# First block: the output projection from rounded halves, in one stage with the second norm

## The reference, cut to what matters

```python
    for i, z in enumerate(branches):
        gate = jax.nn.sigmoid(p[..., GATE_OFF + i * D_MODEL:GATE_OFF + (i + 1) * D_MODEL])
        term = gate * (z @ w_branch[i])
        y = term if y is None else y + term
    return y @ w_out
...
        x = x + mod[2] * _mixer_merge(p, ml_x, *mix_args)
        h = _modulate(_rmsnorm(x, norm2_g[l]), mod[3], mod[4])      # h * (1 + scale) + shift
        x = x + mod[5] * _peer(h, *peer_args)
```

## Time and profile before

| | |
|---|---|
| median of three runs | 4560.39 us (4550.98 to 4560.59) |
| the profiled execution | 4564.81 us, span 4563.0 us |
| TensorE busy | 4219.2 us (92%) |
| DVE busy | 2528.1 us (55%) |
| ScalarE busy | 1668.1 us (37%) |
| POOL busy | 453.7 us (10%) |
| mean DMA rate | 169 GB/s |
| mean granted TensorE clock | 0.952 of full |

### The profile page before, as it was taken

The page is one execution under the profiler, slowest core; times in us unless marked ns, Lnnn a source line. Parts: engine busy times, 40 slices in busy tenths (PEclk is TensorE's granted clock), DMA queues, the critical chain, the costliest instruction groups (busy, mean ns, idle before and its releaser), DMA issues. The chain is left out here.

```text
span 4563.0 us, 62458 instructions
## 1 busy us (share of the span) xinstructions
PE 4219.2 (92%) x25458; PEld 3636.0 (80%) x25458; DVE 2528.1 (55%) x5099; ACT 1668.1 (37%) x2099; POOL 453.7 (10%) x130
## 2 busy tenths in 40 slices
PE   5899889999999999999979798999998988898788
PEld 4777468888887888888778598998887977887687
DVE  4635359766661344444475477764666645553664
ACT  2333133333332322222245244444444433443453
POOL 1222024300000000000034150000000012000000
PEclk7999989999999999999989899999998989998999
DMA  6421123445558765555444355778886511545164
GB/s 220 157 92 60 72 76 120 138 148 185 185 177 306 239 211 186 202 185 201 160 126 133 134 167 182 247 249 283 284 287 216 163 44 56 153 158 165 56 188 136
DMA packets 453479, 769.75 MB, mean 169 GB/s; under 512 B 20389, under 2 KB 324741, under 8 KB 432937
## 3 DMA queue, kind: packets, MB, share of 16 engines
q1 hardware_dynamic: 452554, 763.65, 50.0%
q10 hardware_dynamic: 640, 2.11, 0.1%
HBM read 662.31 MB, written 103.38 MB: 168 GB/s over the span
## 5 line engine op out<-in xcount | busy, mean ns | idle before, releaser
L113 PE MATMUL bank<-hThi_l,pr_whi 128*128 128x512 f32 (+1 forms) x2304 | 788.7, 342 | 30.9 <-DVE pr_wlo L1787 15.7
L113 PE MATMUL bank<-hTlo_l,pr_whi 128*128 128x512 f32 (+1 forms) x2304 | 777.8, 338 | 0.0
L113 PE MATMUL bank<-hThi_l,pr_wlo 128*128 128x512 f32 (+1 forms) x2304 | 777.8, 338 | 0.0
L113 PE MATMUL bank<-pr_whi,pr_ahi 128*128 128x512 f32 x1536 | 600.8, 391 | 10.0 <-DVE pr_alo L1886 9.7
L1692 ACT ACTIVATE pr_whi<-pr_w 128x2048 fp32r<-128x2048 f32 x270 | 515.5, 1909 | 245.3 <-DMA pr_w<-peer_v_in 237.8
L113 PE MATMUL bank<-pr_whi,pr_alo 128*128 128x512 f32 x1536 | 599.3, 390 | 0.0
L113 PE MATMUL bank<-pr_wlo,pr_ahi 128*128 128x512 f32 x1536 | 599.3, 390 | 0.0
L113 PEld LDWEIGHTS bank<-hThi_l,pr_whi 128*128 128x128 f32 x2304 | 440.7, 191 | 81.2 <-DVE pr_wlo L1787 17.1
L113 PEld LDWEIGHTS bank<-hThi_l,pr_wlo 128*128 128x128 f32 x2304 | 440.4, 191 | 45.6
L113 PEld LDWEIGHTS bank<-hTlo_l,pr_whi 128*128 128x128 f32 x2304 | 441.1, 191 | 43.3
L1872 DVE TENSOR_TENSOR pr_a<-pr_gs,pr_g 128x1024 f32<-128x1024 f32 (+1 forms) x128 | 122.7, 959 | 489.8 <-DMA pr_g<-dense_weights 489.8
(11 more groups left out here) (545 smaller groups left out, 8296.6 us busy)
## 6 DMA issues: line engine op xcount, KB each, us to landing
pr_w<-peer_u_in SPq DMA_DIRECT2D x128, 1024.0 KB, 5.7
pr_w<-peer_v_in SPq DMA_DIRECT2D x128, 1024.0 KB, 5.0
dense_weights<-pr_buf SPq DMA_DIRECT2D x12, 4096.0 KB, 17.0
gu_w<-ffn_w_up_in SPq DMA_DIRECT2D x88, 512.0 KB, 4.8
gr_w<-w_in_in SPq DMA_DIRECT2D x32, 1024.0 KB, 5.3
expert_scores<-pr_s SPq DMA_DIRECT2D x64, 512.0 KB, 6.8
pr_gs<-expert_scores SPq DMA_DIRECT2D x64, 512.0 KB, 5.9
pr_g<-dense_weights SPq DMA_DIRECT2D x64, 512.0 KB, 7.1
```

What stands on the lines that cost most here:

```text
L113: ins = pe.matmul(psum, a, b, start=first and i == 0, stop=last and i == len(terms) - 1)
```

## The change

`project` and `norm` between mixing and retrieval are replaced by one stage, `merge_out`. y and w_out become pairs of halves. w_out is cut into four quarters of 256 columns, and a product tile is one quarter by one row tile: 16 tiles in layer 0, 8 in layer 1. The four quarters are fetched at the end of the mixing stage; the high halves of quarters 0 and 1, the low half of quarter 0 and the high halves of y are made there too, the others in the new stage. TensorE does quarters 0 and 1 for all row tiles first, then quarters 2 and 3 row tile by row tile; behind each row tile DVE and ScalarE norm it, while TensorE goes on. The shift and scale rows are fetched when the first half of the tiles is ready; the gain and the weights of the retrieval stage at the stage's start.

In the mixing stage:

```diff
-                for n in range(11, n_w):
+
+                fetch_branch(11)
+                sp.wait_ge(gate_psum, halves_n - 4)
+                fetch_out(0, out_in0)
+                fetch_branch(12)
+                sp.wait_ge(gate_psum, halves_n - 2)
+                fetch_out(1, out_in1)
+                fetch_branch(13)
+                sp.wait_ge(gate_psum, halves_n)
+                fetch_out(2, out_rest)
+                sp.wait_ge(gated, n_it)
+                fetch_out(3, out_rest)
+                for n in range(14, n_w):
                     fetch_branch(n)
                 sp.wait_ge(mod_in, 32)
+                sp.wait_ge(out_rest, 32)
+                sp.wait_ge(out_lo, 1)
...
+                pool.wait_ge(out_hi, 1)
+                pool.tensor_tensor(room.lo[0], room.raw[0], room.hi[0].bitcast(F32), ALU.subtract).then_inc(out_lo, 1)
...
+                    if i == halves_n - 1:
+                        act.wait_ge(out_in0, 16)
+                        act.activation(room.hi[0], room.raw[0], ACT.Copy).then_inc(out_hi, 1)
...
+                act.wait_ge(out_in1, 16)
+                act.activation(room.hi[1], room.raw[1], ACT.Copy).then_inc(out_hi, 1)
+                for o in range(KD):
+                    act.wait_ge(added, halves_n - 16 + o + 1)
+                    act.activation(room.y_hi[:, o, t0:TALL], yT[:, o, t0:TALL], ACT.Copy)
```

`fetch_out(n, landed)` fetches quarter n of w_out, 1 MB, into `room.raw[n]`. The new stage (its opening and small helpers are cut; `bank` cycles through PSUM banks 0 to 3, `turn_bank` through 4 to 7):

```diff
+def merge_out(K, l, x, y, room, mod2, gain2, hT, tiles, streams, ahead):
...
+    items = [(n, t) for n in range(2) for t in tiles] + [(n, t) for t in tiles for n in range(2, 4)]
+    half = 2 * n_t
...
+        @block.sync
+        def _(sp):
+            sp.dma_start(gain2, K.dram["norm2_g"][l:l + 1, :].broadcast_to([P, D])).then_inc(gain_in, 16)
+            ahead.fetch(sp, first_in, rest_in)
+            sp.wait_ge(ready, half)
+            for c in (1, 0):
+                for s in streams:
+                    sp.dma_start(room.mods[:, c, s, :], K.ada[l, s:s + 1, (3 + c) * D:(4 + c) * D].broadcast_to([P, D])).then_inc(mods_in, 16)
+            ahead.land(sp, first_in, rest_in)
...
+            def high_terms(i):
+                n, t = items[i]
+                if n:
+                    pe.wait_ge(w_low, n)
+                if i >= 4:
+                    pe.wait_ge(freed, i - 3)
+                for k in range(KD):
+                    left = y_hi[:, k, t * P:(t + 1) * P]
+                    pe.matmul(bank(i), left, room.hi[n][:, k, :], start=k == 0, stop=False)
+                    pe.matmul(bank(i), left, room.lo[n][:, k, :], start=False, stop=False)
+
+            def low_term(i):
+                n, t = items[i]
+                for k in range(KD):
+                    if i == 0:
+                        pe.wait_ge(y_low, k + 1)
+                    last = pe.matmul(bank(i), y_lo[:, k, t * P:(t + 1) * P], room.hi[n][:, k, :], start=False, stop=k == KD - 1)
+                last.then_inc(ready, 1)
+
+            def turn(j):
+                for g in range(2 * j, 2 * j + 2):
+                    pe.wait_ge(scaled, g + 1)
+                    if g >= 4:
+                        pe.wait_ge(lo_done, g - 3)
+                    for c in range(4):
+                        at = (4 * (g % 2) + c) * P
+                        last = pe.transpose(turn_bank(g)[:, c, :], h[:, j % 2, at:at + P], K.ident[:, :])
+                    last.then_inc(turned, 1)
+
+            high_terms(0)
+            high_terms(1)
+            low_term(0)
+            low_term(1)
+            for i in range(2, len(items)):
+                high_terms(i)
+                low_term(i)
+                j, odd = divmod(i - half, 2)
+                if j >= 2 and not odd:
+                    turn(j - 2)
+            for j in range(n_t - 2, n_t):
+                turn(j)
...
+            def split_hi(n):
+                act.activation(room.hi[n], room.raw[n], ACT.Copy).then_inc(w_high, 1)
+
+            def square(j):
+                act.wait_ge(added, half + 2 * j + 2)
+                act.activation(h[:, j % 2, :], x[:, tiles[j], :], ACT.Square, scale=D ** -0.5, accum_out=ss[:, j:j + 1]).then_inc(squared, 1)
+
+            def root(j):
+                act.wait_ge(shifted, j + 1)
+                act.activation(ss[:, j:j + 1], ss[:, j:j + 1], ACT.Sqrt).then_inc(rooted, 1)
+
+            def hi_of(j):
+                for g in range(2 * j, 2 * j + 2):
+                    act.wait_ge(turned, g + 1)
+                    at = place(g)
+                    act.activation(hT[0][:, at[0], at[1]], turn_bank(g), ACT.Copy).then_inc(hi_done, 1)
+
+            split_hi(2)
+            split_hi(3)
+            ahead.split_hi(act, first_in, ahead_hi)
+            for j in range(n_t):
+                if j >= 2:
+                    hi_of(j - 2)
+                square(j)
+                root(j)
+            for j in range(n_t - 2, n_t):
+                hi_of(j)
...
+            def split_lo(n):
+                if n >= 2:
+                    dve.wait_ge(w_high, n - 1)
+                dve.tensor_tensor(room.lo[n], room.raw[n], room.hi[n].bitcast(F32), ALU.subtract).then_inc(w_low, 1)
+
+            def take(i):
+                n, t = items[i]
+                dve.wait_ge(ready, i + 1)
+                if i >= 4:
+                    dve.wait_ge(added, i - 3)
+                part = K.junk[:, i % 4 * 256:(i % 4 + 1) * 256]
+                dve.tensor_tensor(part, bank(i), mod2[:, t // 2, cols(n)], ALU.mult).then_inc(freed, 1)
+                dve.wait_ge(freed, i + 1)
+                dve.tensor_tensor(x[:, t, cols(n)], x[:, t, cols(n)], part, ALU.add).then_inc(added, 1)
+
+            def lo_of(j):
+                for g in range(2 * j, 2 * j + 2):
+                    dve.wait_ge(hi_done, g + 1)
+                    at = place(g)
+                    dve.tensor_tensor(hT[1][:, at[0], at[1]], turn_bank(g), hT[0][:, at[0], at[1]].bitcast(F32), ALU.subtract).then_inc(lo_done, 1)
+
+            def scale_row(j):
+                t = tiles[j]
+                dve.wait_ge(squared, j + 1)
+                dve.tensor_scalar_add(ss[:, j:j + 1], ss[:, j:j + 1], EPS).then_inc(shifted, 1)
+                if j == 0:
+                    ahead.split_lo(dve, ahead_hi)
+                dve.wait_ge(rooted, j + 1)
+                chain(dve.reciprocal(ss[:, j:j + 1], ss[:, j:j + 1]))
+                for c in range(2):
+                    part = slice(c * 512, (c + 1) * 512)
+                    chain(dve.scalar_tensor_tensor(out=h[:, j % 2, part], in0=x[:, t, part], scalar=ss[:, j:j + 1], in1=scale[:, t // 2, part],
+                                                   op0=ALU.mult, op1=ALU.mult))
+                    dve.tensor_tensor(h[:, j % 2, part], h[:, j % 2, part], shift[:, t // 2, part], ALU.add).then_inc(scaled, 1)
+
+            for k in range(KD):
+                dve.tensor_tensor(y_lo[:, k, t0:TALL], yT[:, k, t0:TALL], y_hi[:, k, t0:TALL].bitcast(F32), ALU.subtract).then_inc(y_low, 1)
+            split_lo(1)
+            for i in range(half):
+                take(i)
+                if i in (n_t - 2, half - 2):
+                    split_lo(2 if i < n_t else 3)
+            dve.wait_ge(gain_in, 16)
+            dve.wait_ge(mods_in, 32 * len(streams))
+            for s in streams:
+                last = dve.scalar_tensor_tensor(out=scale[:, s, :], in0=scale[:, s, :], scalar=1.0, in1=gain2, op0=ALU.add, op1=ALU.mult)
+            chain(last)
+            for j in range(n_t):
+                take(half + 2 * j)
+                take(half + 2 * j + 1)
+                if j >= 2:
+                    lo_of(j - 2)
+                scale_row(j)
+            for j in range(n_t - 2, n_t):
+                lo_of(j)
```

More of the change, by code:

```diff
@@ L731, in mixers @@
+def mixers(K, l, hT, zTs, yT, shared, qk, vones, gates, osig, y, gm, ft, tiles, streams, held, room):
     nc = K.nc
@@ L861, in _, with fetch_out @@
                         fetch_branch(n - 5)
-                for n in range(11, n_w):
+                def fetch_out(n, landed):
+                    sp.dma_start(room.raw[n], K.dram["w_out"][l][:, n * 256:(n + 1) * 256].rearrange("(k p) n -> p k n", p=P)).then_inc(landed, 16)
+                fetch_branch(11)
[10 more added lines that the diff above has]
+                for n in range(14, n_w):
                     fetch_branch(n)
                 sp.wait_ge(mod_in, 32)
+                sp.wait_ge(out_rest, 32)
+                sp.wait_ge(out_lo, 1)
             @block.gpsimd
```

72 lines of the change are left out of this document (51 added, 21 removed).

## The result

| | before | changed kernel |
|---|---|---|
| median | 4555.97 us (4 runs, 4550.98 to 4560.59) | 4530.11 us (4 runs, 4524.88 to 4531.19) |
| ratio, 95% interval | 1 | 0.994 (0.9928 to 0.9952) |
| span of the profiled execution | 4563.0 us | 4529.3 us |

The change takes 25.9 us off the median (22 to 33 by the interval); forecast were 42 us, and a time of 4518 us. The spans of the two profiled executions differ by 33.7 us. The table of stretches of the changed kernel, in order: tail, stage to the request for the mod rows, to their arrival, to the end, all layer 0; then tail and stage of layer 1. Columns are those of the earlier trace rows.

What follows compares the result with a forecast made beforehand. TensorE was busy 92% of the span and stages did not overlap, so its waits and slow work set the time. Gains of 25.6 us (layer 0) and 15.9 (layer 1), called 42, took 4560.4 to 4518; range 4502 to 4535.

Steps and rivals of the forecast that it cites:

- Products at 0.118 us: New stage: 128x256 products start 0.118 us apart, 2.85 us a tile of 24; product form alone worth 14 us.
- Rival (b): New stage: products do not overlap and cost 0.285 us each; layers lose 26 and 12 us, time 4598; chance 0.03.
- (a): New stage: TensorE falls to the low clock, 0.236 us a product; layers lose 7 and 2 us, time 4570; chance 0.05.
- First half: Layer 0's new stage: product tiles of the first two quarters, the last of them, tile 7, ready at 23.1 us.
- Mod rows: Layer 0's new stage: shift and scale rows, requested when tile 7 is ready, take 7.5 us for 2 MB.
- Row tiles: Layer 0's new stage, after the scale products: DVE's chain sets the pace, 8.4 us for the first, then 6.45 each.
- Cold start, 2.5 us: Start of layer 0's new stage: TensorE at the low clock for 5.5 us or so, tile 7 and later 2.5 us late.
- Layer 1's stage: New stage of layer 1: 35.0 us, with the modulation rows arriving at 16.6 us and a 2.3 us tail.
- Branch weights of layer 1, 3 us, ends 0 and 6: Layer 1's mixing stage: moved w_out fetches go ahead of branch weights 14 and 15, delaying TensorE 3 us (0 to 6).
- ScalarE's other additions are hidden: Mixing stage: ScalarE's added copies, 1.9 us for the first quarter, fit its idle time before the last gate; cost 0.
- POOL's 4.8 us start behind that copy and end before the branch products do: Mixing stage: GpSimd's 4.8 us of work follows ScalarE's copy of the first quarter and costs nothing.
- Rival (c): New stage: DVE chain longer through hand-overs, modulation rows 3 us later, table loads at roots; gain 28, time 4532; chance 0.18.

Runs made afterwards that it cites:

- tail_both: Changed kernel, but VectorE instead of GpSimd makes quarter 0's low half, earlier, and quarter 3 is requested behind the last branch weights: 4514.63 us, ratio 0.9907.
- all_three: tail_both's edits on the changed kernel, plus mod rows requested behind the first quarter's tiles, ahead of all retrieval weights but the first: 4513.16 us, ratio 0.9894.
- out3_late: Changed kernel with quarter 3 of the projection weights requested behind the last two branch weights instead of ahead of them: 4528.69 us, ratio 0.9942.
- pool_pieces: Changed kernel with GpSimd's low half of quarter 0 cut into four instructions of a quarter of its size: 4528.28 us (one run).

## Why the prediction was right, and where it was not

The sign, the mechanism and the range held (4502 to 4535; 4530.11 measured). The time is 12 us above the forecast and just outside the case's own range (4510 to 4528). The gain is 16 us short of 42: with a fourth run the median of the kernel before came out 4.4 us lower than the 4560.39 that the forecast started from, so the time lies 4.4 us nearer to its forecast than the gain does, and that is luck. In the profiled executions the stretches gave 31.6 us where the steps summed to 41.5. Step by step:

- **Products at 0.118 us.** Measured 0.12 us between starts, as in these rows of layer 0's second half, so 2.88 us for 24 against 2.85:

```profile
555.58 0.28 PE L797 MATMUL bank<-mr_lo,mr_yhi 128*128 128x256 f32 x1
555.70 0.28 PE L796 MATMUL bank<-mr_hi,mr_yhi 128*128 128x256 f32 x1
555.82 0.28 PE L797 MATMUL bank<-mr_lo,mr_yhi 128*128 128x256 f32 x1
```

  Rival (b) is dead, and so is (a): the clock was 1.00 to 554.56 and 0.87 behind it, where TensorE is not the bound. What the Trainium skill, TensorE: Matmul & The Clock Gate, says of cycling through PSUM banks in another, bf16, kernel does not show here: 1.00 over the 32.6 us of product tiles ahead of VectorE's scale products. Behind them the clock did swing (0.66 from 565 to 570, 1.00 from 570 to 580), but there TensorE also stood still for VectorE (3.21 us ahead of 563.84), so these rows do not single out the banks.
- **First half.** Tile 7 was ready 23.66 us in (23.1).
- **Mod rows.** 8.98 us from request to use (7.5), so 1.5 us under-sized. The scale products cost 2.36 + hand-over, as forecast.
- **Row tiles.** 8.14 and three times 6.3 (8.4 and 6.45), one table load. The tail behind the last row was 2.95 us (2.3). Stage: 65.0 against 63 + 2.5. That this fits to 0.5 us is partly luck: the cold start of 2.5 us did not come, and the mod rows (1.5), the first half (0.6) and the tail (0.65), all put too low, took its place.
- **Cold start, 2.5 us.** It did not come in the changed kernel. It did in tail_both and all_three (0.57 in the first 4 us) and in out3_late (0.60); in tail_both it cost 1.2 us up to the mod rows' request. Right in kind, half the size.
- **Layer 1's stage.** 36.6 against 35.0: mod rows at 17.95 us (16.6) and a longer tail.
- **Branch weights of layer 1, 3 us, ends 0 and 6.** In the changed kernel TensorE waited only 0.28 and 0.48 us for them, since the transposes were later. Without the lock it waits 5.04 us. The term was near the top of its range, but hidden.
- **The step that failed**: "ScalarE's other additions are hidden" and "POOL's 4.8 us start behind that copy and end before the branch products do". Both are true of the engines that do the work. I asked whether GpSimd had time, and not what its instruction does to VectorE beside it. The last terms of layer 0, one copy of 0.6 us, are what tail_both shows (0.62 us above before). Lock and traffic together added 4.5 us in layer 0 (24.31 against 19.78 in tail_both), of which 3.0 go with the lock alone. In layer 1 they made the tail 4.2 us longer than my 3.4 over before, partly through the clock, which fell behind TensorE's 4.16 us of standing still.

These make up the 9.9 us but for rounding: tails +4.5 and +4.2, stages -0.5 and +1.6. Rival (c) gave 4532, close to the measured time, but not by what happened: VectorE's chain was as short as forecast, and there was no second table load. That its number fits is chance.

The trace of before had the warning, in a place off the critical path that I did not read:

```profile
382.81 0.69 DVE L1245 TENSOR_TENSOR junk<-bank,mx_gate 128x512 f32<-128x512 f32 x1 [6.27 <-PE bank L919]
383.51 4.51 POOL L870 TENSOR_TENSOR gr_wlo<-gr_w,gr_whi 128x2048 fp32r<-128x2048 f32 x1 [14.79 <-ACT gr_whi L1077]
383.54 5.03 DVE L1247 TENSOR_TENSOR yT_l<-yT_l,junk 128x512 f32<-128x512 f32 x1
```

An add of 0.69 us that takes 5.03, beside the same kind of GpSimd instruction. The same happens at four more gates of that layer (5.02 to 5.11 us), each time beside a GpSimd low half. A table by line hides it in a mean; the shortest and longest duration of one line shows it at once.

The Trainium skill, SBUF — State Buffer, "SBUF: two separate sides", calls the port pair that VectorE and GpSimd share an exclusive lock: a VectorE instruction with two SBUF inputs and a GpSimd one that reads SBUF exclude each other, and whichever starts first holds the pair for its whole length. By that rule the add should take the 4.61 us of GpSimd's instruction and its own 0.69, 5.3 us less the 0.02 between their starts. The trace agrees to 0.15 us (5.13), and for one piece in pool_pieces the same sum gives 1.95 against 1.82 measured.

## What to carry to other kernels

When work is moved to an idle GpSimd, list the VectorE instructions with two SBUF operands that run in that time and what stands behind them: the price is theirs, up to GpSimd's whole instruction each. Place it where VectorE idles behind one such instruction, or let VectorE do it (2.3 us instead of 4.6). And where two late arrivals end the same wait, an experiment on one alone can show almost nothing (in layer 1 here 1.3 and 1.2 us, no more than the scatter, against 5.9 together in tail_both and 2.1 in all_three, where the clock fell); look at what the engine waits for next in the edited run before giving a cause up.

## What was not expected of the hardware

- The hold goes instruction by instruction, and the engines alternate: four GpSimd pieces took 5.83 us instead of 4.61, so GpSimd is held up as well, and cost VectorE 1.1 us for the add and 3.0 over the four products behind it.
- Whether a short stop of TensorE costs clock varies between nearly equal places: 2.53 us of standing still ahead of layer 0's new stage left the clock at 1.00 in the changed kernel and at 0.57 in tail_both; in layer 1, 2.15 us left it at full and 3.17 us brought it to the lower level, which made 16 matmuls 2.8 us longer than those of tail_both. Those 3.17 us of waiting cost 6.0 us in all. What decides between the two outcomes these runs do not show.
